# A hybrid encoder on one core: latent sums, two weight splits, one square and one sine in other places of the order

## What is computed

```
for l in range(DEPTH):
    h = rmsnorm(x, norm_mix_g[l])
    proj = h @ w_in[l]
    h_q, h_kv, k_pe, h_sg = proj[..., :c1], proj[..., c1:c2], proj[..., c2:c3], proj[..., c3:]
    o_mla = mla_mixer(...)
    o_sg = spatial_gating_mixer(...)
    o = concatenate([rmsnorm(o_mla, ...), rmsnorm(o_sg, ...)])
    x = x + o @ w_out[l]
    x = x + memory_attention(rmsnorm(x), rmsnorm(mem), ...)
    x = x + conv_ffn(rmsnorm(x), ...)
return rmsnorm(x, final_norm_g)
```

## Time and profile before

| what | value |
|---|---|
| median of 3 runs | 1486.0 us (1485.4 to 1487.34) |
| the profiled execution, its own time | 1485.25 us |
| its span, first to last instruction | 1483.5 us |
| TensorE busy | 1455.1 us, 98% of the span |
| VectorE, ScalarE, GpSimd busy | 49%, 47%, 46% |
| mean granted clock of TensorE | 0.995 of full speed |

### The profile page before, as it was taken

One profiled execution on the slowest core, in us unless ns is written; L12 is line 12 of the kernel. 1 busy time (PEld: TensorE's weight loads), 2 busy tenths in 40 slices (PEclk: granted clock), 3 DMA queues, 4 the chain that ended last, 5 costly groups with the idle time before them and its releaser, 6 DMA issues.

```text
span 1483.5 us, 19468 instructions
## 1 busy us (share of the span) xinstructions
PE 1455.1 (98%) x6872; PEld 1197.7 (81%) x6872; DVE 734.2 (49%) x1123; ACT 698.5 (47%) x1134; POOL 682.9 (46%) x343
## 2 busy tenths in 40 slices
PE   9999999999999999999999999999999999999997
PEld 7777689888888888888878777988888888888885
DVE  7648579353455410545254776771535544024533
ACT  6578556353344422444355885553534444224432
POOL 2545358534443454354445543684344354435351
PEclk9999999999999999999999999999999999999998
DMA  5320225412232333232323102463022332323231
GB/s 202 117 71 15 72 90 170 139 44 73 72 107 90 113 101 98 86 108 79 119 82 102 55 29 86 128 185 99 15 99 60 112 113 86 113 86 101 74 95 57
DMA packets 38889, 138.76 MB, mean 94 GB/s; under 512 B 4448, under 2 KB 4704, under 8 KB 38560
## 3 DMA queue, kind: packets, MB, share of 16 engines
q1 hardware_dynamic: 37296, 133.20, 28.6%
q10 hardware_dynamic: 1520, 4.56, 0.9%
HBM read 135.64 MB, written 2.10 MB: 93 GB/s over the span
## 4 chain that ended last, share of the span: by engine, by line
PE 77%; issue 10%; DVE 5%; POOL 4%; ACT 4%; DMA 0%; SPq 0%; POOLq 0%; DVEq 0%
PE ps L1470 25%; PE ps L1472 25%; PE ps L1471 25%; POOL w_lo L377 4%; PE ps L1628 1%; ACT work L664 1%; DVE small L1162 1%; ACT h_hi L743 0%; DMA raw<-blocks_d 0%; ACT arena L672 0%; DVE arena L1328 0%; ACT h_hi L752 0%; DVE arena L1188 0%; DVE work L1005 0%; PE ps L1659 0%
## 5 line engine op out<-in xcount | busy, mean ns | idle before, releaser
L377 POOL TENSOR_TENSOR w_lo<-raw,w_hi 128x1024 fp32r<-128x1024 f32 x244 | 593.7, 2451 | 663.3 <-ACT w_hi L512 663.3
L512 ACT ACTIVATE w_hi<-raw 128x1024 fp32r<-128x1024 f32 x247 | 255.0, 1054 | 326.6 <-PE ps L1472 323.9
L1470 PE MATMUL ps<-h_hi,w_hi 128*128 128x512 f32 (+1 forms) x1040 | 406.1, 390 | 1.8 <-DVE h_lo L1058 1.0
L1472 PE MATMUL ps<-h_hi,w_lo 128*128 128x512 f32 (+1 forms) x1040 | 403.1, 388 | 0.0
L1471 PE MATMUL ps<-h_lo,w_hi 128*128 128x512 f32 (+1 forms) x1040 | 403.1, 388 | 0.0
L1470 PE MATMUL ps<-arena,w_hi 128*128 128x512 f32 (+1 forms) x648 | 240.8, 372 | 0.0
L1472 PE MATMUL ps<-arena,w_lo 128*128 128x512 f32 (+1 forms) x648 | 238.8, 369 | 0.0
L1471 PE MATMUL ps<-arena,w_hi 128*128 128x512 f32 (+1 forms) x648 | 238.6, 368 | 0.0
L1470 PEld LDWEIGHTS ps<-h_hi,w_hi 128*128 128x128 f32 x1040 | 195.3, 188 | 45.2 <-issue 3.2
L1471 PEld LDWEIGHTS ps<-h_lo,w_hi 128*128 128x128 f32 x1040 | 195.3, 188 | 40.7 <-issue 1.0
L1472 PEld LDWEIGHTS ps<-h_hi,w_lo 128*128 128x128 f32 x1040 | 195.3, 188 | 40.2
(11 more groups left out here) (200 smaller groups left out, 1815.6 us busy)
## 6 DMA issues: line engine op xcount, KB each, us to landing
raw<-blocks_d SPq DMA_DIRECT2D x247, 512.0 KB, 3.5
work<-memT_d ACTq DMA_DIRECT2D x2, 1024.0 KB, 4.8
x<-xT_d SPq DMA_DIRECT2D x3, 512.0 KB, 7.9
work<-ln_d ACTq DMA_DIRECT2D x2, 512.0 KB, 3.6
outT_d<-work SPq DMA_DIRECT2D x4, 256.0 KB, 2.5
outT_d<-work ACTq DMA_DIRECT2D x4, 256.0 KB, 2.7
x<-xT_d SPq DMA_DIRECT2D x2, 256.0 KB, 4.8
raw<-blocks_d SPq DMA_DIRECT2D x2, 256.0 KB, 5.1
```

The costliest lines, as they stand in the source:

```text
L377: gp.tensor_tensor(w_lo[:, b % SPLIT, :], raw[:, b % RAW, :], w_hi[:, b % SPLIT, :].bitcast(F32), ALU.subtract).then_inc(lo_done.sem, 1)
L512: act.activation(w_hi[:, b % SPLIT, :], raw[:, r, :], ACT.Copy).then_inc(hi_done.sem, 1)
L1470: pe.matmul(out, a_hi, b_hi, start=first, stop=False)
L1472: return pe.matmul(out, a_lo, b_hi, start=False, stop=last)
```

## The change

It has four parts.

1. The sine and its table load stand behind the last tile of the opening, and not behind the split of tile 6.
2. `latent_sums` is called ahead of the third block of u (`at=2`), and not ahead of the second.
3. The splits of the third and fourth output blocks (`ahead(B_V + 7)`, `ahead(B_OUT)`) stand behind the last output square, and not in steps (6, 2) and (7, 0).
4. The second output square stands in step (6, 0) and its addition in (6, 1), each one step sooner.

```diff
--- before.py
+++ after.py
@@ -100,8 +100,8 @@
 GATED_VAR, GATED_ROOT = (5, 3), (6, 0)
 SCALED_STEP = (6, 1)
 
-SQUARE_STEPS = ((4, 3), (6, 1), (7, 1))
-ADD_STEPS = ((6, 2), (7, 2))
+SQUARE_STEPS = ((4, 3), (6, 0), (7, 1))
+ADD_STEPS = ((6, 1), (7, 2))
 
 
 class Signal:
@@ -580,14 +580,13 @@
                             split_first()
                         elif t % 2 == 0:
                             split(t // 2)
-                        if t == 6:
-                            act.wait_ge(trig_dve, 1)
-                            act.activation(turn_q[64:128, 0, :], work[64:128, 0, :], ACT.Sin).then_inc(trig_act, 1)
                         if t == 1:
                             square(0, MIX, 0)
                         if t >= 1:
                             square(0, MIX, t)
                     act.sem_inc(x_ready.sem, x_ready.start)
+                    act.wait_ge(trig_dve, 1)
+                    act.activation(turn_q[64:128, 0, :], work[64:128, 0, :], ACT.Sin).then_inc(trig_act, 1)
                 else:
                     for b in range(AHEAD):
                         split(b)
@@ -733,10 +732,8 @@
                             k_even((h + 2) // 2)
                         else:
                             k_second((h + 2) // 2)
-                    if t == 2 and h in (2, 4, 6):
+                    if t == 2 and h in (2, 4):
                         ahead(B_V + 4 + h // 2)
-                    if (h, t) == (7, 0):
-                        ahead(B_OUT)
                     for c in range(TT):
                         if (h, t) == STAT_STEPS[c]:
                             need(vmean, 1)
@@ -761,6 +758,8 @@
                 gate_turned(3)
                 copy_sums(HEADS - 1)
                 square_output(3)
+                ahead(B_V + 7)
+                ahead(B_OUT)
 
                 act.dma_start(memT, memT_d).then_inc(mem_in.sem, 16)
                 wide_root(MLA, 0)
@@ -1566,7 +1565,7 @@
                         cols=[slice(0, 128), slice(128, 256), slice(256, 384), slice(320, 448)],
                         between=mixers_norm)
                 need(s_v, 1)
-                project_tokens(B_U, BA, h_hi, h_lo, lambda k: None, between=latent_sums, at=1)
+                project_tokens(B_U, BA, h_hi, h_lo, lambda k: None, between=latent_sums, at=2)
 
                 block_ready(B_WV)
                 wh, wl = halves(B_WV, 512)
```

## The result

| kernel | median | runs | ratio to before |
|---|---|---|---|
| before | 1485.74 us | 1485.4 to 1487.34 (4 runs) | 1 |
| after | 1499.05 us | 1498.44 to 1502.51 (4 runs) | 1.0092 (1.0075 to 1.011) |

The forecast was 1501.1 us with a range from 1492 to 1504, slower with a chance of 0.9. The change costs 13.3 us.

The account below looks back on a forecast made before the run. TensorE, busy in 98% of the span, was taken to bound the kernel. Terms 0 + 9.0 + 2.9 - 0.1 + 3.3 = +15.1 us on the profiled 1485.25 gave 1500.4, as a median 1501.1 us, range 1492 to 1504.

Parts of the forecast that it names:

- The sine: Opening: moving the table load and sine on ScalarE frees nobody, since VectorE's squares end the opening; 0 us.
- The shift: Latent sums a block later: all that hangs on them comes 3.8 us later in the first layer, 5.4 in the second.
- GpSimd's turn: Q scale: VectorE's last product waits behind back-to-back GpSimd low parts, 2.95 us in place of 0.69, +2.3 us.
- Both together: First query projection: delayed sums plus blocked VectorE product, less 2.4 us slack; 3.7 and 5.3 us later, +9.0 us.
- The norm: Behind the last output square: two GpSimd low parts delay the norm's first product, +1.3 and +1.6 us, +2.9 together.
- The square: Last attention steps: square on ScalarE costs 0.5 us, earlier addition on VectorE saves 0.6; -0.1 us in each layer.
- The clock: Behind the two query projection stalls: one fall to 1.2 GHz each, +3.3 us, with the first layer's old fall kept.
- the rival with more idle: Clock stays low for longer or falls at a third place: 1504 us and over, chance 0.08.
- That GpSimd yields: Q scale: VectorE's last product stays free in both layers, 4.6 us less, 1496.5 us, down to 1493; chance 0.2.
- That VectorE is in time: Low parts of v begin once ScalarE's copies are there, so the sums win 1.7 us: 1482.7 us, chance 0.05.

## Why the prediction was right, point by point

- **The sine: 0 forecast, 0 found.** Table load and sine ran from 22.97 to 24.90 in after, in ScalarE's wait for VectorE; the opening's idle was 1.13 us there and 1.08 us in the run of the sine and the square alone. The 2.66 us of the Trainium skill (ScalarE: Activation LUTs, What ACT_TABLE_LOAD costs) for a switch of tables did not show: the load of 1.28 us began 0.02 us behind the square ahead of it, and the sine 0.02 us behind the load.
- **The shift: right mechanism, a bit too large in the first layer.** Forecast were 3.8 and 5.4 us. In the first layer the key copy began at 47.26 and not at 43.80, 3.5 us later; in the second it came 5.4 us later, beyond the 4.8 us by which everything was late there. What was left out is that the two waits of 1.51 and 0.15 us cost TensorE more than their length: from the end of u's block to the next product before took 2.0 us longer than after, and not 1.66, and all of it went with the waits.
- **GpSimd's turn: right, a bit too large.** Forecast were 2.95 us for the last product; it took 2.72. It did end 0.56 us behind GpSimd's instruction (65.14 and 64.58), as the forecast's 0.55 had it. But it began only when that instruction was already under way: one turn of both is 2.72 us (8.16 us for three), and not 2.40 + 0.55. The run with the split of block 11 late showed the term by itself: 2.0 us a layer, where 2.3 had been summed.
- **Both together:** 3.0 and 4.9 us net where 3.7 and 5.3 stood in the sum, stalls of 4.98 and 4.97 us where 5.4 and 5.3 were expected. Of the 2.0 us by which after came out under the forecast, 1.1 are here. Another 1.0 us is in no term: before's profiled execution, from which the rows come, was 0.75 us under its median, and after's was 0.27 us above its own.
- **The norm: right.** +1.3 and +1.6 us forecast, +1.19 and +1.56 found. The run of the fourth block's split alone and the run of the two splits separate the cause: one `w_lo` costs nothing, two cost 2.75 us.
- **The square: right in after.** -0.1 us a layer forecast, -0.10 and -0.13 found by elapsed time; the sum took the term once and not for both layers, 0.1 us. The idle brackets alone give -0.3. The difference fits a wait in two pieces from which TensorE has to pick up twice, which no run shows by itself. Without part 3 the next wait grows by 0.2 us a layer, as the run of the sine and the square showed; the forecast didn't see that the two parts hang together. VectorE's wait for ScalarE grew from 0.68 to 1.20 us, the 0.5 us of the forecast.
- **The clock: right behind the stalls, and in size by luck.** I had counted one fall for each stall, 3.3 us, and kept the old one. Found were 2.39 and 1.33 us behind the stalls, a third fall behind the second layer's norm (1.55 us), and the old one gone (-1.65 us): 3.6 us. Two misses of about the same size cancelled. The fall at a third place was the condition of the rival with more idle; its 1504 us didn't come, since the old fall was gone.
- **The rivals.** That GpSimd yields fell with the three rows of 2.7 us. That VectorE is in time did not happen (the last product of the q scale ended at 65.14), and the run with the low parts first shows what it had needed: another order on VectorE, and not a faster VectorE. With it after's sums cost nothing.

## What to carry over

Before a step is moved later because the busiest engine idles ahead of it, follow what hangs on the step to the next place where that engine waits, and compare the shift with the slack there in each layer: here 1.7 us of idle in one layer were traded for a stall of 5 us in both. Look also at what the move lets start together: here three instructions of GpSimd without a pause made one more instruction of VectorE four times as long, and the cheap remedy was an order in which VectorE works from the partial sums while GpSimd is busy. A step that pays in one layer only is moved in that layer only.

## What the runs showed of the hardware

- VectorE and GpSimd take turns, instruction by instruction, when both queue work with two inputs in SBUF: VectorE's 0.69 us became 2.72 to 2.78 us, three times in a row, while GpSimd's 2.40 us became only 2.72 on average. So in this case nearly all of the cost falls on the engine with the shorter instructions. VectorE's instructions with one input in the partial sums were not held up: in after the four of `v_lo` took 2.48 us together, from 65.17 on, while GpSimd's next instruction ran from 65.52 to 67.89.
- The clock's fall is not a matter of one wait's length alone. In after it fell behind a wait of 2.06 us in the second layer; in the run of the two splits a wait of 2.06 us at the same place, and two of 2.00 us, left it at full speed. A fall of this kind cost 1.3 to 2.4 us in after, and before's own runs spread from 1482.93 to 1487.11 us, more than any of the small gains here; the five at a mean clock of 0.997 took up to 1483.92 us, the seventeen at 0.995 took 1485.10 us and more.
- Whether one wait is cut in two may matter to the clock. In the five traces in which the 2.0 us at the transposes stand in one piece, the clock fell there at five of ten places; in the five in which they stand in two, at none of ten. This is a hint and not shown: the run of the sine and the square, with its two pieces, was no faster than before, and three of its ten executions had a mean clock of 0.995.
